# An encoder layer in six phases: SBUF allocated from both ends, first loads of both attentions and first weights of the merge moved into the phase in front, a third PSUM bank for dense units, fewer semaphore clears

## What is computed

```python
h = rmsnorm(x, norm_g)
(g_q, g_k, g_v, g_lr, z_a, d_q, d_k, d_v, z_b, c_q, z_c, gate_in) = split(h @ w_in)
o_a = gla_branch(g_q, g_k, g_v, g_lr, ...) * silu(z_a)       # gated linear attention, forward scan + backward scan, rmsnorm
o_b = diff_attention(d_q, d_k, d_v, ...) * silu(z_b)         # softmax(s0 + alibi) - lam * softmax(s1 + alibi), 4 heads
o_c = memory_cross_attention(c_q, mem, ...) * silu(z_c)      # 4 heads into 256 memory tokens
gates = sigmoid(gate_in)                                      # 3 x 1024 columns
merged = sum over branches of gates * (o_branch @ w_branch)
y = rmsnorm(x + merged @ w_out, final_norm_g)
```

## Time and profile before

| what | value |
|---|---|
| runs | 3538.6, 3539.0, 3540.56 us, median 3539.0 |
| profiled execution | 3538.0 us, its span 3535.9 us (2.1 us lie around the span) |
| PE / PEld busy | 3370.4 us (95%) / 2625.5 us (74%) |
| DVE / ACT / POOL busy | 58% / 38% / 34% |
| mean granted TensorE clock | 0.982 of full speed |
| DMA | 554.64 MB, mean 157 GB/s |

### The profile page before, as it was taken

One profiled execution on the slowest core, in us unless ns is written; L12 is line 12 of the kernel. 1 busy time (PEld: TensorE's weight loads), 2 busy tenths in 40 slices (PEclk: granted clock), 3 DMA queues, 4 the chain that ended last, 5 costly groups with the idle time before them and its releaser, 6 DMA issues. The chain is left out here.

```text
span 3535.9 us, 46863 instructions
## 1 busy us (share of the span) xinstructions
PE 3370.4 (95%) x16944; PEld 2625.5 (74%) x16944; DVE 2065.7 (58%) x4688; ACT 1329.2 (38%) x2165; POOL 1216.5 (34%) x511
## 2 busy tenths in 40 slices
PE   7999999999999999999999887999999978999998
PEld 5888888877888888888877764666666545888887
DVE  3322312226655665565557778989988745666554
ACT  2111111123333333333333225666666645333332
POOL 2322412333333333333333224776677622100000
PEclk9999999999999999999999998999999989999999
DMA  6545545463453544544348865121221075775662
GB/s 204 177 156 176 178 152 178 163 233 121 136 180 118 179 135 124 169 140 132 114 159 272 296 201 164 57 79 39 72 61 54 23 258 196 247 238 195 202 213 84
DMA packets 318419, 554.64 MB, mean 157 GB/s; under 512 B 35437, under 2 KB 115565, under 8 KB 318190
## 3 DMA queue, kind: packets, MB, share of 16 engines
q1 hardware_dynamic: 266510, 470.74, 40.9%
q10 hardware_dynamic: 51680, 80.91, 6.3%
HBM read 382.03 MB, written 169.50 MB: 156 GB/s over the span
## 5 line engine op out<-in xcount | busy, mean ns | idle before, releaser
L665 POOL TENSOR_TENSOR glaf_w_lo<-early_raw,glaf_w_hi 128x1024 fp32r<-128x1024 f32 x140 | 345.1, 2465 | 711.3 <-ACT glaf_w_hi L639 711.3
L694 PE MATMUL glaf_dense_acc<-h_hi,glaf_w_hi 128*128 128x512 f32 x1120 | 452.0, 404 | 4.1 <-ACT glaf_dense_out L648 4.1
L694 PE MATMUL glaf_dense_acc<-h_lo,glaf_w_hi 128*128 128x512 f32 x1120 | 438.6, 392 | 0.0
L694 PE MATMUL glaf_dense_acc<-h_hi,glaf_w_lo 128*128 128x512 f32 x1120 | 437.0, 391 | 0.0
L1671 DVE CUSTOM_DVE_ANT_0 diff_p<-diff_s_ps,diff_table 128x512 f32<-128x512 f32 x544 | 345.4, 685 | 41.1 <-PE diff_s_ps L1536 39.0
L451 POOL TENSOR_TENSOR proj_w_lo<-early_raw,proj_w_hi 128x1024 fp32r<-128x1024 f32 x84 | 204.4, 2436 | 479.4 <-DVE proj_w_hi L414 479.4
L1497 POOL TENSOR_SCALAR diff_p<-diff_p,diff_ratio 128x1024 f32<-128x1024 f32 (+1 forms) x80 | 270.1, 3376 | 176.6 <-DVE diff_ratio L1691 176.6
L1615 ACT ACTIVATE diff_p<-diff_p,diff_neg_max 128x2048 f32<-128x2048 f32 (+1 forms) x160 | 278.6, 1742 | 41.8 <-DVE diff_neg_max L1681 41.7
L1535 PE MATMUL diff_s_ps<-diff_k,diff_q_high 128*128 128x512 f32 x544 | 246.3, 453 | 40.3 <-DVE diff_mx L1671 23.8
L1560 PE MATMUL diff_oT_ps<-diff_aT,diff_v 128*128 128x512 f32 x544 | 273.7, 604 | 6.0 <-ACT diff_aT L1609 6.0
L1062 DVE COPY_PREDICATED glaf_att<-glaf_picked,glaf_att_ps 128x256 f32<-128x256 int32 x280 | 147.2, 526 | 214.6 <-PE glaf_att_ps L827 207.7
(11 more groups left out here) (215 smaller groups left out, 7369.8 us busy)
## 6 DMA issues: line engine op xcount, KB each, us to landing
early_raw<-in_w_zg SPq DMA_DIRECT2D x180, 512.0 KB, 4.2
early_raw<-in_w_stream SPq DMA_DIRECT2D x80, 512.0 KB, 3.5
scratch_zg<-glaf_dense_out SPq DMA_DIRECT2D x140, 256.0 KB, 2.2
items_raw<-in_w_br SPq DMA_DIRECT2D x120, 256.0 KB, 3.0
merge_gate<-scratch_zg SPq DMA_DIRECT2D x120, 256.0 KB, 3.3
scratch_featT<-proj_out ACTq DMA_DIRECT2D x80, 256.0 KB, 2.2
items_br_hi<-scratch_item_hi SPq DMA_DIRECT2D x60, 256.0 KB, 6.5
items_br_lo<-scratch_item_lo SPq DMA_DIRECT2D x60, 256.0 KB, 7.1
```

The costliest lines, as they stand in the source:

```text
L665: pool.tensor_tensor(self.w_lo[:, s], self.raw[:, u % self.RAW], self.w_hi[:, s], ALU.subtract).then_inc(self.lo_split, 1)
L694: done = pe.matmul(self.acc[:, u % self.BANKS], a, x, start=i == 0, stop=i == self.PER - 1)
```

## The change

SBUF tensors can now be allocated from the right end (`side="right"`; h, `early`, and `front.p` are), so that the next phase's tensors exist beside those of the present one. In the order of the program:

1. `clear()` clears only at the end of diff and of merge (`last=True`), there all semaphores used so far; at the other four ends neither L69 nor L70 is left.
2. The `ones` row of `early.glr` is set by DVE at the start of project, no longer at that of gla forward (L1000).
3. `early.load_w` for the backward phase is issued before the last dense store of the forward phase, not after it.
4. The backward phase's `Dense` has 3 PSUM banks (forward still 2).
5. The backward phase's SP loads q of group 0 at n = 10 (6 DMAs, 768 KB), the first k at n = 12 (4 DMAs, 512 KB), the near table at n = 14 (448 KB) for diff; its POOL sets the zero half of `q_low` after unit 20's low part, with a wait ahead and one behind. In diff these are gone; PE waits for `ones` only at its first sum of squares; lam is computed after the maximum of turn 0.
6. diff's SP waits for the last turns of near and far, then loads what cross needs first (kT, v, q, z for two chunks and both memories, 8 DMAs, 6 MB) into `front.p`, the buffer that held the scores, and only then stores groups 17, 18, 19. In cross these loads are gone; its SP starts with the merge's weights and items.
7. cross splits the merge's first three weights at the end of its iterations n = 10, 11, 12 (`items.high` on ACT, `items.low` on DVE), and merge no longer starts with them.

```diff
-    def block(self):
+    def block(self, used, last=False):
         def clear():
-            self.nc.clear_and_free_semaphores(self.allocated)
-            self.nc.all_engine_barrier()
+            used.extend(self.allocated)
+            if last:
+                self.nc.clear_and_free_semaphores(used)
+                used.clear()
+                self.nc.all_engine_barrier()
...
                 if u >= self.banks:
                     pe.wait_ge(self.evacuated, u - self.banks + 1)
...
 (gla forward, SP)
                 for slot in range(j * PER, (j + 1) * PER):
+                    if slot + 1 == N * PER:
+                        sp.wait_ge(dense.lo_split, dense.count)
+                        early.load_w(sp, 1, w_zg, BACKWARD_UNITS)
                     dense.transfers(sp, slot)
-            sp.wait_ge(dense.lo_split, dense.count)
-            early.load_w(sp, 1, w_zg, BACKWARD_UNITS)
...
 (gla backward, SP)
+                if n == N // 2:
+                    ahead.load_q(sp, 0, 0, slice(0, CH))
+                if n == N // 2 + 2:
+                    ahead.load_k(sp, 0, 0, slice(0, CH))
+                if n == N // 2 + 4:
+                    ahead.load_near(sp)
...
 (gla backward, POOL)
                 dense.low(pool, u)
+                if u == dense.count // 2:
+                    pool.wait_ge(dense.lo_split, u + 1)
+                    ahead.zero(pool)
+                    pool.wait_ge(ahead.zeroed, 1)
...
 (diff, SP, its end)
             load_z(NG - 1)
+            sp.wait_ge(near_done, TURNS)
+            sp.wait_ge(far_done, TURNS)
+            front.load(sp)
             for g in range(NG - 3, NG):
                 store(g)
...
 (cross, ACT; DVE has the same with items.low)
                 if n >= 3 and (n - 3) % TT == TT - 1:
                     output((n - 3) // TT)
+                if 0 <= n - N // 2 < items.SPLIT:
+                    items.high(act, n - N // 2)
```

More of the change, by code:

```diff
@@ L53, in __init__, with sb @@
         self.allocated = []
-    def sb(self, name, shape, dtype=FP32):
-        return self.ctx.enter_context(self.nc.sbuf_tensor(f"{self.phase}_{name}", shape, dtype))
+    def sb(self, name, shape, dtype=FP32, side="left"):
+        return self.ctx.enter_context(self.nc.sbuf_tensor(f"{self.phase}_{name}", shape, dtype, side=side))
     def ps(self, name, shape):
@@ L693, in products_until @@
             x = (self.h_hi, self.h_lo, self.h_hi)[part][:, b, k]
-            done = pe.matmul(self.acc[:, u % self.BANKS], a, x, start=i == 0, stop=i == self.PER - 1)
+            done = pe.matmul(self.acc[:, u % self.banks], a, x, start=i == 0, stop=i == self.PER - 1)
             if i == self.PER - 1:
@@ L1463, in _ @@
             load_k(3)
-            sp.dma_start(table[:, :near.start], alibi_left).then_inc(table_in, 16)
-            sp.dma_start(table[:, near.stop:], alibi_right).then_inc(table_in, 16)
+            ahead.load_far(sp)
             load_z(0)
@@ L1979, in load_w, with high, low @@
             sp.dma_start(self.raw[:, u], self.w_br[u % 3 * KT + u // 3]).then_inc(self.w_in[u], 16)
+    def high(self, act, u):
+        act.wait_ge(self.w_in[u % self.RAW], 16 * (u // self.RAW + 1))
+        act.activation(self.w_hi[:, u % self.SLOTS], self.raw[:, u % self.RAW], ACT.Copy).then_inc(self.hi_split, 1)
+    def low(self, dve, u):
+        s = u % self.SLOTS
+        dve.wait_ge(self.hi_split, u + 1)
+        dve.tensor_tensor(self.w_lo[:, s], self.raw[:, u % self.RAW], self.w_hi[:, s], ALU.subtract).then_inc(self.lo_split, 1)
     def load(self, sp, first, last):
@@ L2142, in wo_split @@
                 act.activation(wo_hi[:, kt], x[:, kt % XS], ACT.Copy).then_inc(wo_high, 1)
-            for u in range(AHEAD):
-                high(u)
             act.preload_act_table(ACT.Sigmoid)
@@ L2250, in scale @@
                 dve.scalar_tensor_tensor(x[:, n % XS], x[:, n % XS], stat[:, n % 2, 2:3], gain[:, :], ALU.mult, ALU.mult).then_inc(normed, 1)
-            for u in range(AHEAD):
-                low(u)
             for c in range(NC):
@@ L2303, in build @@
-        phase_diff(nc, ident_tile, featT, featT_lo, diff_v, alibi, lambdas, diff_gain, zg, item_hi, item_lo)
+        used = []
+        with ExitStack() as ahead_ctx:
+            with ExitStack() as gla_ctx:
+                m = Mem(nc, gla_ctx, "h")
+                h = [m.sb(half, [P, H_BUFFERS, KT, CH], FP32R, side="right") for half in ("hi", "lo")]
+                early = Early(nc, gla_ctx)
+                phase_project(nc, used, h, early, w_zg, w2, ident_tile, x_all, gains, ident, w_stream, w_glr, w_values, w_mem, w_mem_values, hT_hi, hT_lo,
+                              featT, featT_lo, glrT, [gla_v, diff_v], memkT, mem_v)
+                phase_gla_forward(nc, used, h, early, ident_tile, featT, glrT, w2, gla_v, gla_sums, gla_picked, gla_diag, gla_o, qb, kb, decb,
+                                  hT_hi, hT_lo, w_zg, zg)
+                ahead = Ahead(nc, ahead_ctx, featT, featT_lo, alibi)
+                phase_gla_backward(nc, used, h, early, ahead, ident_tile, gla_v, gla_o, qb, kb, decb, gla_gain, item_hi, item_lo, hT_hi, hT_lo, w_zg, zg)
+            front_ctx = ctx.enter_context(ExitStack())
+            front = Front(nc, front_ctx, featT, memkT, mem_v, zg)
+            phase_diff(nc, used, ahead, front, ident_tile, diff_v, lambdas, diff_gain, zg, item_hi, item_lo)
```

254 lines of the change are left out of this document (131 added, 123 removed).

## The result

| | before | changed |
|---|---|---|
| median of the runs | 3539.78 us (4 runs, 3538.6 to 3540.82) | 3564.33 us (4 runs, 3562.62 to 3568.77) |
| ratio, 95% interval | | 1.0071 [1.0054, 1.0089] |
| span of the profiled execution | 3535.9 us | 3560.8 us |

What follows compares the result with a forecast made beforehand. PE, busy 95% of the span, was taken as the bound, so gains come only from its idle places and half clock. Terms summed to -27.5 from 3538.0, giving 3510.5, plus 1.0 for the median: 3511.5 us, range 3504 to 3525.

Steps and rivals of the forecast that it cites:

- the 0.02 for slower: Whole kernel: chance 0.02 of being slower, for an allocation or a queue that no profile row of before shows.
- The third bank, -19.5: Backward phase: a third bank ends PE's waits for DVE's multiply and the half clock after them; -19.5 us.
- All six fall: Backward phase: all six PE waits for DVE's multiply before a dense unit disappear, 14.1 us.
- the 7.3 us for the clock: Backward phase: 14.64 us of PE's work in four half-clock stretches takes half as long at full clock, saving 7.3 us.
- Its own sign of being wrong: Backward phase: a wait for `w_lo` of more than a few us would show the forecast wrong.
- The rival of the weights: Backward phase: late weights take the bank's place, leaving the bank 10 us, total 3521 us; chance 0.25.
- Forward to backward, +1.3: Forward-backward border: the last store lands just behind the four early weight loads, so PE starts later; +1.3 us.
- Backward to diff, -8.8: Diff's start: with q, k and the zeros already there, PE starts right behind the first barrier; -8.8 us.
- Diff to cross, -4.6: Diff-cross border: cross's first 6 MB load before diff ends, so PE starts at 2853.7, not 2858.32; -4.6 us.
- The rival on the other side: End of diff: stores behind 6 MB of loads end diff some 14 us later, total 3525 us; chance 0.03.
- The split in cross, +5.0: Cross: DVE's low parts wait for ACT's high parts and delay the maxima, exp and PE; +5.0 us.
- Merge, -0.7: Merge: unit 4 still waits for its weights, so the moved splits gain nothing and only the clear's 0.7 us is left.

Runs made afterwards that it cites:

- e5: Changed kernel with 352 bytes per partition allocated at the right end in front of h; 3529.85 us, ratio 0.9971.
- e9: e5 with two PSUM banks instead of three for the backward phase's dense units; 3534.58 us, ratio 0.9981.
- e10: Kernel before with a third PSUM bank in the backward phase and nothing else; 3534.07 us, ratio 0.9982.
- e12: e5 with the backward phase's first weights loaded behind the forward phase's last store again; 3529.60 us, ratio 0.9967.
- e14: e11 with the backward phase's first weights loaded behind the forward phase's last store again; 3525.36 us, ratio 0.9954.
- e11: e5 with the merge's first three weight splits back at the start of merge instead of in cross; 3525.28 us, ratio 0.9959.
- e3: Kernel before with 32 bytes in front of h and 32 behind it, so h moves by 32 and the weights by 64; 3577.14 us.
- e2: Kernel before with 32 bytes in front of h, so h and the weights both move by 32; 3539.53 us, ratio 0.9998.

## Why the prediction was wrong, step by step

- **The allocation from both ends: +35 us, not in the sum.** The sum had no term for it, and the 0.02 for slower named "an allocation" without a mechanism. This is the step that failed: the term was put at nothing, and h's new distance of 96 from the weights, modulo 256, costs about 6 ns in each matmul of the dense products. With the distance made good (e5) the change is worth 9.6 us by the medians beside each other, and about 34 us lie between e5 and the changed kernel. Even so e5's 3529.85 us stay above the range's 3525; the next step is why. In a kernel in which PE is busy for 95% of the span, a change of the addresses of what PE reads touches every matmul.
- **The third bank, -19.5: measured -5.8 and -4.9 in the phase** (e5 against e9, e10 against before), 3 to 7 us in the whole. "All six fall" was right: 14.1 us of waits are gone. Wrong was to take a wait's fall for time won: 10.1 us of other waits came, and with them half clock behind them, so that of the 7.3 us for the clock less than half came (half clock for 17.1 us before, 10.3 in the changed kernel, 17.1 in e5). The prediction looked for what is late next and found the weights, with 0.9 us to spare, but judged them by the times of before; the weights are issued behind a store that waits for the same late multiply, so they could not come earlier than DVE lets them. PE's wait for DVE's `total`, the larger of the new ones, was not in it at all. Its own sign of being wrong, a wait for `w_lo` of more than a few us, came true with 4.6 us. The rival of the weights, at 0.25 and 10 us, was the nearest; its mechanism (more loads in the queue) was not the one found.
- **Forward to backward, +1.3: measured +1.8** in the gap, with the store behind the loads. In the whole e12 and e14, whose loads stand behind the store again, are not measurably faster than e5 and e11.
- **Backward to diff, -8.8: measured -8.1** in the gap (8.0 to 9.5 us in all profiles with the early loads but e9's 7.3, 16.2 before). Diff's +1.0 is not clear of the profiles' scatter: the kernel before and its variants have 720.9 to 723.3 us. Lambda's chain of 1.3 us now stands behind turn 0; that it costs PE anything is not shown.
- **Diff to cross, -4.6: measured -3.9.** The 6 MB ahead of the stores cost nothing. The term that was mis-sized is the clear of all semaphores, 1.5 us where 0.6 + 0.25 were taken. The rival on the other side, loads before stores, did not happen: the kernel is slower for another reason.
- **The split in cross, +5.0: measured +2.6** between the two profiles, and up to 5 in others (cross 111.7 to 114.5 us with it, 107.6 to 109.8 without). The mechanism is the one described, DVE waiting for ACT's high part.
- **Merge, -0.7: measured -0.1**, gap and phase together. Unit 4 waits for its weights before as after.
- **Clears and end:** -0.8 and +0.4, about as taken (-0.6 and +0.4).

Without the first two steps the terms add up to -8.0 and what was measured in their place to -7.1. In the prediction's own arithmetic the bank's 21.4 less 2 is 19.4, not 19.5, and the range's upper end, the weights' case at 3521 with +3 for +1.3 at the first border, is 3522.7, not 3525; neither changes the account.

## What to carry to other kernels

Before a tensor that PE reads is moved, write down its address and that of its partner: in this kernel the moving and the loaded operand of a float32r product should lie a multiple of 256 bytes apart, and a pad of 352 bytes restored it. When PE is fully busy at full clock and still slower, count matmuls in equal windows; no view of waits will show it. And when a buffer is added so that an engine need not wait for a late one, follow the queue that feeds it: an in-order queue that stores the late result before it loads the next operands hands the delay on.

## What the runs showed of the hardware that was not expected

The time of a float32r matmul of 128x512 that follows another depends on the distance in SBUF from the loaded operand to its moving one, modulo 256 bytes. In project it is 227 ns on average from start to start at 0 (226 or 227 in nine of ten), 229 at 64, and 232.6 to 234.3 at the others tried: 96, 128 and 224 with h moving, 32, 128, 160 and 192 with h loaded; single steps reach 241. Over the 7,368 matmuls of dense products in the first three phases that is 24 to 39 us between two kernels. Shifting both by 32 bytes changes nothing, nor does the distance as a whole (83 KB before, 175 KB in e5). A distance of 0 is not all that it takes: the score products of diff have the same form, and k at byte 17024 and q_high at 33408 are 0 apart modulo 256, yet one follows the other after 232 ns on average (for example at 2201.38, 2201.61 and 2201.85 us of the kernel before). What slows these was not looked into. The Trainium skill, in "TensorE: Matmul & The Clock Gate", section "Step-by-step: what each phase is for", says that the streaming operand and the weight load have independent read ports and that loading the next weights does not take read bandwidth from the running matmul; by that e3 would be as fast as e2, and the runs, 3577 against 3540 us, decide otherwise for these operands. What in the chip makes the time depend on the distance is open, a collision of the two reads is a guess; other element types and shapes were not tried.
